# Peer routing search: picks in PSUM, 64 candidates per head, a paired first query step and key scores three pieces late

## The chip, the cores and the metric

The kernel runs on one core of one Trainium2 chip. The metric is the device time of one execution in microseconds (us). A core has TensorE (PE, matmuls, with its weight loads shown as PEld), VectorE (DVE), ScalarE (ACT), GpSimd (POOL) and SyncE (SP, which here only starts the transfers of the weight stream). Each engine works through its own instructions in the order in which the program gives them, and semaphores tie the engines together.

## The reference, cut to what matters

Two transformer blocks run one after the other over 256 tokens of width 1024. The change lies in the last part of the second block, a product-key expert layer:

```
def _peer(h, w_q, subkeys, w_down, w_up):        # h: tokens x 1024
    q = (hblk @ w_q).reshape(B, TB, 8, 2, 128)
    s = jnp.einsum('btphd,phnd->btphn', q, subkeys)      # 8 heads x 2 halves x 128 keys
    v, i = lax.top_k(s, 16)
    cand = (v[..., 0, :, None] + v[..., 1, None, :]).reshape(..., 256)
    cidx = (i[..., 0, :, None] * 128 + i[..., 1, None, :]).reshape(..., 256)
    tv, tj = lax.top_k(cand, 16)
    eidx = jnp.take_along_axis(cidx, tj, axis=-1)
    w = jax.nn.softmax(tv, axis=-1)
    a = jax.nn.gelu(jnp.einsum('btd,btpkd->btpk', hblk, w_down[eidx]))
    return jnp.einsum('btpk,btpkd->btd', w * a, w_up[eidx])
```

There are 128 x 128 experts. The kernel does not gather the chosen ones. It computes `gelu(h @ w_down.T)` for all of them in 128 tiles of 128 experts, multiplies each tile by the routing weight of every (expert, token) pair, which is zero where the expert was not chosen, and multiplies by `w_up`.

## The kernel before, in words

All weights come as one stream of 529 pieces of 128 x 1024 float32 (512 KB each), through a ring of three buffers. SP starts the transfer of piece q + 3 when the low part of piece q is done. Each piece is split into a rounded high part `wh` (ACT, L201) and a low part `wl` = piece - `wh` (L208, on DVE or, with `low=G`, on POOL). PE multiplies with three products per tile: high x high, low x high, high x low (`mm3`, L253 to L255). Three buffers of `wh` and `wl` exist (`AHEAD = 3`): ACT may write the high part of piece q + 3 only after PE has used piece q (semaphore `s_used`), and PE may start piece q only when `s_low` says that its low part is there. A piece of the query projection or of a `down` tile is 24 matmuls of 256 columns (8 slices k of the contraction x 3 products).

The part that the change touches runs in this order on PE.

1. **Operand.** `rms_operand(1, ...)` normalizes x, turns it and makes the high and low operand `xh`, `xl`, two slices k at a time (L360, L362, L366, L372). Only then, after `release()`, does POOL start the transfer of the 1 MB of sub-keys (`ld_keys`, L142).
2. **Query stage.** The loop at L1944 has 17 steps. Step st does the query piece `ph = st` (`feature_piece`, 24 matmuls into bank 0 or 1), ACT copies the result to `qp` (L1954), then PE multiplies the queries of `ph = st - 1` with their 128 sub-keys (4 instructions in the rows for the two token blocks, L1962), ACT copies the scores (L1966) and DVE searches the 16 largest of 128 for each of the two token blocks (`max`, `max_index`, `match_replace`, `max`, `max_index`: L1971 to L1978). After the loop PE waits for all score copies.
3. **Lead tiles.** 36 `down` tiles (`lead_tile`) follow, of which 0 to 5 are written out, 6 to 29 run in a loop and 30 to 35 are written out. ACT applies the gelu (L2003). The low parts of this stage and of the query stage are made by POOL. Meanwhile DVE does the routing: index conversion (L2021), sums of 16 x 16 candidates per head (L2028), top 16 of 256 for 8 heads x 2 token blocks (L2031 to L2038), softmax pieces (L2042, ACT's exp L2045), places split into row and column (L2047 to L2050), and then the picks: for row and column, and for each token block, a compare with 0..15 (L2060), a multiply by the indices (L2062) and a sum (L2064), each over 2048 elements per partition, all in SBUF. The exp stands in ACT's order behind the loop, that is behind the gelu of tile 29. Then come the sum of the weights, the reciprocal and the scaling (L2066 to L2071).
4. **Turn.** Before tile 33 PE transposes the picked indices and the weights (`turn_route`, L2078), ACT copies them out (L2081), and DVE makes the one-hot tiles (L2102, L2103).
5. **Route loop.** From the end of tile 35 on, 64 groups of four tokens are expanded by PE (L2120) beside 64 more `down` tiles, with the low parts made by DVE. Then the remaining tiles are weighed and multiplied with `w_up`.

## Time and profile before

| what | value |
|---|---|
| median of 3 runs | 1870.27 us (1869.08 to 1873.82) |
| the profiled execution, its own time | 1867.74 us |
| its span, first to last instruction | 1866.4 us |
| mean granted TensorE clock | 0.974 |
| busy: PE / DVE / ACT / POOL | 1751.0 / 1282.6 / 903.4 / 231.9 us |
| operand stage and query stage | 983.75 to 1054.5 us |
| lead tiles until the turn | 1054.5 to 1159.2 us |

Busy times are shares of a span with many stages, so they do not say which engine sets the end of one stage. That is read from stretches of the span and from the order of the instructions in the stretch. A granted clock of 1.00 is TensorE's level of 2.4 GHz, 0.50 that of 1.2 GHz.

### The profile page before, as it was taken

The page shows a single profiled execution, that of the slowest core. Times are in us where ns is not written, and L with a number is a line of the kernel's source. Part 1 is how long each engine was busy: PE and PEld are TensorE (multiplying, and loading weights), DVE is VectorE, ACT ScalarE, POOL GpSimd, SP SyncE. Part 2 cuts the span into 40 slices and gives each one's busy share as a digit, 9 for nine tenths or more (in the row PEclk, how much of TensorE's full clock was granted, in tenths as well). Part 3 has the DMA queues.
Part 4 walks back from the last instruction along what each step waited for, and adds up shares of the span by engine and source line. Part 5 has one row for each costly group of instructions (what it writes and reads, how often), then busy time and mean ns, then how long its engine had stood idle before and what let it go on. Part 6 is the DMA issues. An engine that isn't in the chain of part 4 may idle for free.

```text
span 1866.4 us, 31955 instructions
## 1 busy us (share of the span) xinstructions
PE 1751.0 (94%) x11408; PEld 1573.2 (84%) x11408; DVE 1282.6 (69%) x2300; ACT 903.4 (48%) x1584; POOL 231.9 (12%) x147
## 2 busy tenths in 40 slices
PE   7988999989989999898887998999999999999997
PEld 6757998768879987797777998999999998888885
DVE  5376866775768666767655998777786666666665
ACT  4734443455544434546444444777774443333332
POOL 1020000001110000022103799100000000000000
PEclk9989999999999999999988999999999999999999
DMA  7534756644536675444223454444445555555553
GB/s 270 199 112 138 263 180 239 237 158 145 170 119 237 216 255 194 140 147 136 80 90 114 154 173 153 146 143 137 146 138 165 184 186 185 187 186 190 191 184 120
DMA packets 85893, 317.56 MB, mean 170 GB/s; under 512 B 9568, under 2 KB 9840, under 8 KB 85024
## 3 DMA queue, kind: packets, MB, share of 16 engines
q1 hardware_dynamic: 76464, 278.43, 44.6%
q10 hardware_dynamic: 7776, 26.50, 4.0%
q0 software_dynamic: 1552, 11.25, 1.6%
q8 instruction: 67, 1.10, 0.2%
q14 instruction: 34, 0.28, 0.1%
HBM read 315.08 MB, written 1.05 MB: 169 GB/s over the span
## 4 chain that ended last, share of the span: by engine, by line
PE 77%; DVE 8%; ACT 5%; issue 4%; DMA 3%; POOL 3%; POOLq 0%; ACTq 0%; SPq 0%; DVEq 0%
PE bank L253 23%; PE bank L255 22%; PE bank L254 22%; PE bank L2120 3%; POOL wl L208 2%; DVE wl L208 2%; ACT wh L201 2%; DMA ada<-in_w_ada 1%; PE bank L493 1%; DMA ring<-in_stream 1%; PE bank L346 1%; PE bank L563 1%; PE bank L528 1%; DVE ada L334 1%; PE bank L527 0%
## 5 line engine op out<-in xcount | busy, mean ns | idle before, releaser
L201 ACT ACTIVATE wh<-ring 128x1024 fp32r<-128x1024 f32 x529 | 559.0, 1059 | 778.0 <-PE bank L255 702.8
L208 DVE TENSOR_TENSOR wl<-ring,wh 128x1024 fp32r<-128x1024 f32 x477 | 583.8, 1227 | 448.6 <-ACT wh L201 448.5
L253 PE MATMUL bank<-xh,wh 128*128 128x256 f32 x2072 | 599.1, 289 | 14.2 <-POOL wl L208 7.3
L255 PE MATMUL bank<-xh,wl 128*128 128x256 f32 x2072 | 589.3, 284 | 0.0
L254 PE MATMUL bank<-xl,wh 128*128 128x256 f32 x2072 | 589.2, 284 | 0.0
L253 PEld LDWEIGHTS bank<-xh,wh 128*128 128x128 f32 x2072 | 400.7, 193 | 20.7 <-issue 9.1
L254 PEld LDWEIGHTS bank<-xl,wh 128*128 128x128 f32 x2072 | 400.4, 193 | 1.2
L255 PEld LDWEIGHTS bank<-xh,wl 128*128 128x128 f32 x2072 | 399.9, 193 | 0.0
L253 PE MATMUL bank<-wh,wa_high 128*128 128x512 f32 x512 | 202.4, 395 | 2.1 <-DVE weighted L2139 1.4
L255 PE MATMUL bank<-wh,wa_low 128*128 128x512 f32 x512 | 201.9, 394 | 0.0
L254 PE MATMUL bank<-wl,wa_high 128*128 128x512 f32 x512 | 201.9, 394 | 0.0
L253 PE MATMUL bank<-wh,xh 128*128 128x256 f32 (+1 forms) x400 | 133.5, 334 | 25.4 <-DVE wl L208 10.7
L208 POOL TENSOR_TENSOR wl<-ring,wh 128x1024 fp32r<-128x1024 f32 x52 | 145.1, 2806 | 32.7 <-ACT wh L201 32.5
L254 PE MATMUL bank<-wl,xh 128*128 128x256 f32 (+1 forms) x400 | 129.7, 324 | 0.0
L255 PE MATMUL bank<-wh,xl 128*128 128x256 f32 (+1 forms) x400 | 129.3, 323 | 0.0
L253 PEld LDWEIGHTS bank<-wh,wa_high 128*128 128x128 f32 x512 | 96.6, 189 | 24.0 <-DVE weighted L2139 1.6
L255 PEld LDWEIGHTS bank<-wh,wa_low 128*128 128x128 f32 x512 | 96.4, 188 | 22.3
L254 PEld LDWEIGHTS bank<-wl,wa_high 128*128 128x128 f32 x512 | 96.4, 188 | 21.6 <-issue 0.2
L253 PEld LDWEIGHTS bank<-wh,xh 128*128 128x128 f32 x400 | 78.6, 197 | 36.0 <-DVE wl L208 12.6
L142 POOL DMA_DIRECT2D ring<-in_g_final x1 | 0.6, 573 | 667.8 <-DVE wl L208 667.8
L255 PEld LDWEIGHTS bank<-wh,xl 128*128 128x128 f32 x400 | 78.6, 197 | 5.4
L254 PEld LDWEIGHTS bank<-wl,xh 128*128 128x128 f32 x400 | 78.9, 197 | 5.1 <-issue 0.2
(417 smaller groups left out, 2316.0 us busy)
## 6 DMA issues: line engine op xcount, KB each, us to landing
ring<-in_stream SPq DMA_DIRECT2D x529, 512.0 KB, 3.4
ada<-in_w_ada ACTq DMA_DIRECT2D x48, 512.0 KB, 4.4
rows<-in_rows POOLq DMA_DIRECT2D x1, 2560.0 KB, 10.7
con<-in_early POOLq DMA_DIRECT2D x1, 2078.0 KB, 9.1
rows<-in_rows POOLq DMA_DIRECT2D x2, 1024.0 KB, 5.6
x_feature_major<-in_x_fm ACTq DMA_DIRECT2D x4, 256.0 KB, 8.0
x<-in_x_tm POOLq DMA_DIRECT2D x1, 1024.0 KB, 7.9
weighted<-in_subkeys POOLq DMA_DIRECT2D x1, 1024.0 KB, 8.3
```

Of the source, the lines that this page charges most:

```text
L142: engine.dma_start(dst, src).then_inc(sem, 16)
L201: C.activation(wh[q % AHEAD][:, :], ring[slot][:, :], ACT.Copy).then_inc(s_high, 1)
L208: low.tensor_tensor(wl[q % AHEAD][:, :], ring[slot][:, :], wh[q % AHEAD][:, :], ALU.subtract).then_inc(s_low, 1)
L253: T.matmul(o, left[0], right[0], start=start, stop=False, skip_group_check=True)
L254: T.matmul(o, left[0], right[1], start=False, stop=False, skip_group_check=True)
L255: return T.matmul(o, left[1], right[0], start=False, stop=stop, skip_group_check=True)
L334: ada["done"].append(dve.did(V.tensor_tensor_reduce(out=t[:, :], in0=t[:, :], in1=ada["silu_c"][:, :], scale=1.0, scalar=0.0, op0=ALU.mult ...
L346: last = T.transpose(dst_banks[k // 2][:, (k % 2) * S + t * P:(k % 2) * S + (t + 1) * P], src[:, t, k * P:(k + 1) * P], ident)
L493: T.matmul(o, v[0], w[:, 0:S], start=first, stop=False, skip_group_check=True)
L528: scored = pe.did(T.matmul(b[:, P:3 * P], q[:, P:2 * P], k, start=True, stop=True, skip_group_check=True))
L563: last = T.transpose(b[:, c * P:(c + 1) * P], pr[u % 3][:, c * P:(c + 1) * P], ident)
L2120: last = T.matmul(bank[g % 4][:, k * P:(k + 1) * P], oh_i[g % 2][:, k, :], oh_j[g % 2][:, k, :], start=True, stop=True, skip_group_check=True)
```

## The change

- **Query stage.** Query pieces 0 and 1 run as a pair: for each slice k PE does the three products of both pieces, and only then goes on to the next slice. The low parts of the two pieces that are prepared behind the pair are made by DVE, later ones by POOL as before. The queries rotate through banks 0, 1 and 7 and through four `qp` tiles. The key scores of head half ph run three pieces behind its query piece, so the loop has 19 steps, of which the last three do the lead tiles 0, 1 and 2 in place of a query piece.
- **Candidates.** With both score lists sorted, only pairs whose rank product allows it can be among the 16 largest sums. The change takes 64 of the 256 pairs: row 0 with 16 columns, rows 1 to 3 with 8, rows 4 to 7 with 4, rows 8 to 15 with 1. The row scores are read from bank 7, into which ACT copies them after tile 5 (where ACT waits for the end of the key search); ACT also converts the key indices there.
- **Places.** A place among 64 is turned into its row (`order`) and column (`place`) by 15 DVE instructions of 256 elements, in place of two shifts and masks and a conversion.
- **Picks.** The 2048-element work tile of the picks lies in PSUM banks 0 to 3, and the places that it is compared with in bank 7. The softmax subtraction comes behind the picks.

The diff, cut:

```diff
+    QB = [bank[0], bank[1], bank[7]]
+    def feature_pair(dst):
+        q = pos["q"]
+        T.wait_ge(s_low, q + 2)
+        for k in range(KD):
+            need_x(k)
+            for i in range(2):
+                h, l = wh[(q + i) % AHEAD], wl[(q + i) % AHEAD]
+                last = mm3(dst[i], (h[:, k * P:(k + 1) * P], l[:, k * P:(k + 1) * P]), (xh[:, k, :], xl[:, k, :]),
+                           k == 0, k == KD - 1)
+                if k == KD - 1:
+                    last.then_inc(s_used, 1)
+        pos["q"] = q + 2
+        split(q + AHEAD)
+        split(q + 1 + AHEAD)
+        return (s_used, q + 2)
-    for st in range(2 * PH + 1):
+    for st in range(2 * PH + 3):
         ph = st
+        if ph == 0:
+            pair_done = feature_pair([QB[0][:, 0:S], QB[1][:, 0:S]])
+        elif 2 <= ph < 2 * PH:
+            pe.wait(moved.get(ph - 3))
+            if ph == 2:
+                G.wait_ge(s_low, pos["q"] + AHEAD)
+            y = feature_piece(QB[ph % 3][:, 0:S], low=G)
+        elif ph >= 2 * PH:
+            lead_tile(ph - 2 * PH, None)
         if ph < 2 * PH:
-            act.wait(y, scored.get(ph - 2))
-            moved[ph] = act.did(C.activation(qp[ph % 2], b[:, 0:S], ACT.Copy))
-        ph = st - 1
+            act.wait(y if ph >= 2 else pair_done, scored.get(ph - 4))
+            moved[ph] = act.did(C.activation(qp[ph % 4], QB[ph % 3][:, 0:S], ACT.Copy))
+        ph = st - 3
...
-    pe.wait(*copied.values())
...
-    for u in range(BODY):
+    for u in range(3, BODY):
         lead_tile(u, None)
+    act.wait(moved[2 * PH - 1], top[2 * PH - 1])
+    rows = bank[7].rearrange("p (n w k) -> p n w k", w=2, k=TOPK)
+    turned_in = act.did(C.activation(bank[7], V16.rearrange("p t n k -> p (t n k)"), ACT.Copy))
+    ci = act.did(C.activation(I16f, I16, ACT.Copy))
...
-    ci = dve.did(V.tensor_copy(I16f, I16))
+    NC_ = 64
+    for lo, n_a, n_b in ((0, 1, 16), (1, 3, 8), (4, 4, 4), (8, 8, 1)):
+        m = dve.did(V.tensor_tensor(cand[:, :, at:at + n_a * n_b].rearrange("p n (a b) -> p n a b", b=n_b),
+                                    rows[:, :, 0, lo:lo + n_a].unsqueeze(3).broadcast_to([P, NT * PH, n_a, n_b]),
+                                    cols[:, :, 1, 0:n_b].unsqueeze(2).broadcast_to([P, NT * PH, n_a, n_b]), ALU.add))
...
+    place, order = bank[7][:, 0:S], bank[7][:, S:2 * S]
+    also = bank[0][:, 0:S]
+    m = dve.did(V.tensor_copy(place, TJ.rearrange("p n k -> p (n k)")))
+    m = dve.did(V.tensor_scalar(count, place, 16.0, None, ALU.is_ge))
+    for edge in (24.0, 32.0, 40.0, 44.0, 48.0, 52.0):
+        m = dve.did(V.scalar_tensor_tensor(count, place, edge, count, ALU.is_ge, ALU.add))
+    m = dve.did(V.scalar_tensor_tensor(order, place, -48.0, count, ALU.add, ALU.max))
...
-    c3 = cand.rearrange("p h (a b) -> p (h a) b", a=TOPK)
+    c3 = banks[:, 0:4 * HALF].rearrange("p (n k) -> p n k", k=TOPK)
+    c4 = banks[:, 0:4 * HALF].rearrange("p (h k a) -> p h k a", h=PH, a=TOPK)
-            pos_ = ABf[:, w, t, :, :].rearrange("p h k -> p (h k)").unsqueeze(2).broadcast_to([P, PH * TOPK, TOPK])
+            pos_ = places[w][:, t * P:(t + 1) * P].unsqueeze(2).broadcast_to([P, PH * TOPK, TOPK])
             m = dve.did(V.tensor_tensor(c3, pos_, io16, ALU.is_equal))
             m = dve.did(V.tensor_tensor(c4, c4, idx_, ALU.mult))
             picked = dve.did(V.tensor_reduce(IJ[:, w, t, :, :], c4, AX.X, ALU.add))
+    s1 = dve.did(V.tensor_tensor(W3, TV, TV[:, :, 0:1].broadcast_to([P, NT * PH, TOPK]), ALU.subtract))
+    act.wait(s1)
+    e_ = act.did(C.activation(Wt, Wt, ACT.Exp))
```

## Rows read from the trace of the kernel before

**Rows 1.** Windows: length, busy PE, PEld, DVE, ACT, POOL; clock, DMA share, GB/s

```profile
991.30:994.70 3.40, 3.40 (x16) 3.21 (x16) 2.71 (x4) 1.42 (x3) 0.64 (x1) 0.51 0.02 5
...
997.90:1002.46 4.56, 0.13 (x2) 0.03 (x1) 0.00 (x0) 1.33 (x2) 3.30 (x2) 0.91 0.78 291
1002.46:1008.60 6.14, 6.14 (x29) 6.14 (x30) 3.03 (x16) 0.38 (x1) 0.00 (x0) 0.51 0.28 93
1008.60:1054.50 45.90, 44.40 (x373) 44.02 (x371) 40.35 (x213) 22.82 (x43) 32.51 (x14) 1.00 0.44 146
1054.50:1107.50 53.00, 52.91 (x438) 52.68 (x439) 50.72 (x164) 24.46 (x36) 45.42 (x18) 1.00 0.52 172
1107.50:1159.10 51.60, 44.29 (x356) 42.82 (x355) 47.53 (x17) 22.61 (x33) 50.89 (x16) 1.00 0.43 144
...
1175.00:1403.00 228.00, 228.00 (x1939) 228.00 (x1938) 177.98 (x298) 170.16 (x486) 0.00 (x0) 1.00 0.42 140
```

**Rows 2.** Timeline of PE: start, length, instruction, count, idle time before

```profile
990.06 0.35 PE L253 MATMUL bank<-xh,wh 128*128 128x256 f32 x1 [1.70 <-DVE xl L372]
...
997.75 0.28 PE L255 MATMUL bank<-xh,wl 128*128 128x256 f32 x1
...
1053.32 0.71 PE L1962 MATMUL bank<-weighted 128*128 128x128 f32 x4 [1.03 <-ACT weighted L1954]
1054.55 0.35 PE L253 MATMUL bank<-xh,wh 128*128 128x256 f32 x1 [0.52 <-ACT weighted L1966]
...
1159.25 0.82 PE L2078 MATMUL bank<-keep,weighted 128*128 128x128 f32 x6
```

**Rows 3.** Waits, 985 to 1062 us: who for whom, total, times, longest

```profile
PE bank L1962 <- DMA weighted<-in_subkeys: 4.4, 1, 4.4
```

**Rows 4.** Waits, 1062 to 1175 us

```profile
ACT wh L201 <- DMA ring<-in_stream: 28.8, 11, 3.4
...
PE bank L253 <- POOL wl L208: 7.3, 7, 1.3
```

**Rows 5.** Timeline of POOL, lead tiles

```profile
1105.32 2.40 POOL L208 TENSOR_TENSOR wl<-ring,wh 128x1024 fp32r<-128x1024 f32 x1 [0.42 <-ACT wh L201]
1108.20 49.34 POOL L208 TENSOR_TENSOR wl<-ring,wh 128x1024 fp32r<-128x1024 f32 x14 [0.48 <-ACT wh L201]
```

**Rows 6.** Chain that ended last, in order of time: sub-keys, one step's scores

```profile
994.07 8.26 DMA weighted<-in_subkeys
...
1018.64 0.44 PE bank L1962 x4
```

**Rows 7.** Single lines: duration ns min/median/max, first and last start us

```profile
L2062 DVE TENSOR_TENSOR weighted<-weighted x4: 4358/4365/4385, 1110.4 to 1143.8; 128x2048 f32<-128x2048 f32 x4
```

**Rows 8.** Timeline around one POOL instruction: DVE reads a bank beside it

```profile
841.35 1.02 POOL L556 TENSOR_SCALAR ss_p<-ss_p,ss_rec 128x256 f32<-128x256 f32 x1 [9.46 <-DVE ss_rec L551]
841.48 0.68 DVE L1425 TENSOR_TENSOR rope_n<-bank,con 128x512 f32<-128x512 f32 x1
```

**Rows 9.** Timeline of DVE: searches of 128 and of 256, picks, weights

```profile
1056.73 0.28 DVE L1971 MAX8 weighted<-weighted 128x8 f32<-128x128 f32 x1
...
1058.30 0.28 DVE L1971 MAX8 weighted<-weighted 128x8 f32<-128x128 f32 x1
...
1084.32 0.43 DVE L2031 MAX8 weighted<-weighted 128x8 f32<-128x256 f32 x1
...
1086.58 0.41 DVE L2031 MAX8 weighted<-weighted 128x8 f32<-128x256 f32 x1
...
1108.04 2.29 DVE L2060 TENSOR_TENSOR weighted<-weighted,keep 128x2048 f32<-128x2048 f32 x1
...
1153.40 4.29 DVE L2071 TENSOR_TENSOR weighted<-weighted 128x128 f32<-128x128 f32 x2
```

**Rows 10.** Timeline of ACT: the exp behind tile 29

```profile
1150.91 1.28 ACT L2045 ACT_TABLE_LOAD   x1
1152.20 0.42 ACT L2045 ACTIVATE weighted<-weighted 128x256 f32<-128x256 f32 x1
```

More of the change, by code:

```diff
@@ L143, in load @@
         return (sem, 16)
-    bank = [base.enter_context(nc.psum_tensor(f"bank{i}", [P, HALF], F32))[:, :] for i in range(8)]
+    banks = base.enter_context(nc.psum_tensor("bank", [P, 8 * HALF], F32))
+    bank = [banks[:, i * HALF:(i + 1) * HALF] for i in range(8)]
     keep = sb(base, "keep", [P, KEEP["_size"]])
@@ L1935, in build @@
     ld_keys = load(G, keys, a["subkeys"], "subkeys")
-    qp = [carve(S) for i in range(2)]
+    qp = [carve(S) for i in range(4)]
     sc1 = [carve(NT, NE) for i in range(2)]
@@ L1941, in build, with down, products @@
     I16f = carve(NT, 2 * PH, TOPK)
+    s_gelu = nc.alloc_semaphore("gelu_done")
+    q0 = pos["q"] + 2 * PH
+    def down(q, s, u, n, first=False):
+        if not first:
+            T.wait_ge(s_gelu, n + (u - 2))
+        def products(h, l):
+            for k in range(KD):
+                last = mm3(bank[4 + u % 3][:, 0:S], (h[:, k * P:(k + 1) * P], l[:, k * P:(k + 1) * P]),
+                           (xh[:, k, :], xl[:, k, :]), k == 0, k == KD - 1)
+            return last
+        piece_ops(q, s, products)
@@ L1942, in build, with lead_tile @@
+    def lead_tile(u, i):
+        n = 0 if i is None else i * BODY
+        down(q0 + u, n, u, n, first=i is None and u < 3)
+        split(q0 + u + AHEAD, i, low=G)
+        C.wait_ge(s_used, n + (q0 + u + 1))
+        row = WA[:, u, :] if i is None else WA[:, bass.ds(n + u, 1), :].rearrange("p a t -> p (a t)")
+        C.activation(row, bank[4 + u % 3][:, 0:S], ACT.Gelu_apprx_tanh).then_inc(s_gelu, 1)
     top = {}
     moved, scored, copied = {}, {}, {}
-    for st in range(2 * PH + 1):
-        ph = st
-        if ph < 2 * PH:
-            b = bank[ph % 2]
-            pe.wait(moved.get(ph - 2))
-            if ph == 0:
-                G.wait_ge(s_low, pos["q"] + AHEAD)
-            y = feature_piece(b[:, 0:S], low=G)
-            act.wait(y, scored.get(ph - 2))
-            moved[ph] = act.did(C.activation(qp[ph % 2], b[:, 0:S], ACT.Copy))
-        ph = st - 1
+    QB = [bank[0], bank[1], bank[7]]
@@ new lines, in feature_pair @@
+    def feature_pair(dst):
+        q = pos["q"]
+        T.wait_ge(s_low, q + 2)
+        for k in range(KD):
+            need_x(k)
[9 more added lines that the diff above has]
+        return (s_used, q + 2)
@@ L1961, in build @@
         for t in range(NT):
-            last = T.matmul(b2[:, t * P:(t + 1) * P], qp[ph % 2][:, t * P:(t + 1) * P], keys[:, ph, :],
+            last = T.matmul(b2[:, t * P:(t + 1) * P], qp[ph % 4][:, t * P:(t + 1) * P], keys[:, ph, :],
                             start=True, stop=True, skip_group_check=True)
@@ L2039, in build @@
-    dve.wait(m)
-    for t in range(NT):
-        s1 = dve.did(V.tensor_tensor(Wt[:, t, :, :], TV[:, t, :, :], TV[:, t, :, 0:1].broadcast_to([P, PH, TOPK]),
-                                     ALU.subtract))
-    act.wait(s1)
-    e_ = act.did(C.activation(Wt, Wt, ACT.Exp))
-    V.tensor_scalar(AB[:, 0, :, :, :], TJ, 4, None, ALU.logical_shift_right)
-    m = dve.did(V.tensor_scalar(AB[:, 1, :, :, :], TJ, TOPK - 1, None, ALU.bitwise_and))
-    dve.wait(m)
-    m = dve.did(V.tensor_copy(ABf, AB))
@@ new lines, in build @@
+    dve.wait(m)
+    for n in range(NT * PH):
+        m = dve.did(V.max(TV[:, n, 0:8], cand[:, n, :]))
+        dve.wait(m)
+        V.max_index(TJ[:, n, 0:8], TV[:, n, 0:8], cand[:, n, :])
+        m = dve.did(V.match_replace(cand2, TV[:, n, 0:8], cand[:, n, :], -3.0e38))
+        dve.wait(m)
+        m = dve.did(V.max(TV[:, n, 8:16], cand2))
+        dve.wait(m)
+        m = dve.did(V.max_index(TJ[:, n, 8:16], TV[:, n, 8:16], cand2))
+    dve.wait(m)
+    place, order = bank[7][:, 0:S], bank[7][:, S:2 * S]
@@ new lines, in build @@
+    dve.wait(m)
+    V.tensor_scalar(also, order, 4.0, 24.0, ALU.mult, ALU.add)
+    m = dve.did(V.tensor_scalar(start_, order, 8.0, 8.0, ALU.mult, ALU.add))
+    dve.wait(m)
+    m = dve.did(V.scalar_tensor_tensor(start_, order, 16.0, start_, ALU.mult, ALU.min))
+    dve.wait(m)
+    m = dve.did(V.scalar_tensor_tensor(start_, order, 48.0, start_, ALU.add, ALU.min))
+    dve.wait(m)
+    m = dve.did(V.tensor_tensor(start_, also, start_, ALU.min))
+    dve.wait(m)
+    m = dve.did(V.tensor_tensor(place, place, start_, ALU.subtract))
```

56 lines of the change are left out of this document (15 added, 41 removed).

## The prediction, made blind

> **What bounds the kernel now.** I read the windows of the second block first, then PE's own timeline at their edges, then the waits, and last the instructions of DVE and POOL one by one. Times "at" are us from the start of the span of before.
>
> In the route loop and behind it PE is busy for 228.00 of 228.00 us at clock 1.00 [rows 1]. Nothing there waits, so whatever the stretch ahead of it saves should arrive at the end in full. What can be saved is where PE is idle or slow between 990 and 1160. A piece or tile of 24 matmuls takes 2.88 us at full clock: low parts that POOL makes in step with PE start at 1105.32 and 1108.20 [rows 5]. The key scores of one step take 0.44 [rows 6]. By this rule 16 query pieces and their scores need 16 x 2.88 + 16 x 0.44 = 53.1 us. They take from 990.06 to 1054.55, 64.5 us [rows 2]. The 11.4 us over are four things. The first two pieces end at 997.87 (the last matmul begins at 997.75, and matmuls follow each other by 0.12) [rows 2], 7.8 us in place of 5.8, because the operand comes two slices at a time and the clock is at 0.51 from 991.3 to 994.7 [rows 1]: 2.0 us. Then PE stands until 1002.46 for the sub-keys [rows 1, 3], whose transfer starts at 994.07 and takes 8.26 [rows 6]: 4.6 us. After this pause the clock is at 0.51, the 1.2 GHz level, for 6.14 us [rows 1], in which one score step and one piece run that need 3.32 at full clock: 2.8 us. At the end the last score step waits for ACT's copy (1.03), runs 0.71 in place of 0.44, and tile 0 waits 0.52 for the last score copy [rows 2]: 1.8 us. The rest of the stage has no gap: 44.40 busy of 45.90 us, nearly all of the rest being this end [rows 1].
>
> The 33 lead tiles up to the turn need 33 x 2.88 = 95.0 us and take from 1054.55 to 1159.25 = 104.7 [rows 2]. The 9.7 us over lie behind 1107.5, where PE is busy 44.29 of 51.60 us, against 52.91 of 53.00 ahead of it [rows 1]. There POOL is the bound: 14 low parts take 49.34 us, 3.52 each against 2.40 alone [rows 5], which is 14 x (3.52 - 2.88) = 9.0 us. PE's own waits name POOL for 7.3 us; ACT waits 28.8 us for ring transfers [rows 4], which start only when a low part is done, so they are late because POOL is. POOL is late because DVE and POOL exclude each other when a DVE instruction has two inputs in SBUF: the multiply of the picks takes 4.37 us every time [rows 7], where the first compare, which came before POOL's instruction, takes 2.29 for as many elements [rows 9].
>
> **The change, part by part.**
>
> *Pair.* PE has 12 matmuls for each two slices of the operand in place of 6, so it fills the waits. At 0.12 us up to 991.3 it does 10 of its 48, at 0.213 (16 in 3.40 us [rows 1]) up to 994.7 another 16, then 22 at 0.12: end at 997.34, 0.5 us sooner. Behind it ACT and DVE make two pieces in a row: high parts end near 998.3 and 999.3, low parts near 999.6 and 1000.8. Piece 2 is ready and runs to 1000.22, piece 3 starts there (margin 0.6 us), piece 4 at 1003.5. DVE has no search yet, so these two low parts delay nothing.
>
> *Scores three pieces late.* PE now does pieces 2 and 3, to 1003.1, before it needs the sub-keys, which were there at 1002.46. Waiting (4.6) and the slow clock behind it (2.8) are gone. The margin is only 0.6 us. From the first scores, at 1003.54 done, 15 steps of 2.88 + 0.44 follow: 12 query pieces and tiles 0, 1, 2, to 1053.3. The last score steps are covered by tiles, so the 1.8 us at the end are gone too. DVE needs 2 x 1.57 = 3.15 us for the two searches of a step [rows 9], under 3.32, so it is through at about 1057, not later than before. Sum of the stage: 0.5 + 4.6 + 2.8 + 1.8 = 9.7 us.
>
> *ACT waits for the key search behind tile 5.* Behind this wait on ACT stand two copies (some 1.2 us) and the high part and gelu of tile 6, and behind them POOL and PE. ACT comes there at 1053.3 + 3 x 2.88 + 1.4 = 1063.4, 6 us after DVE is through: no cost. The two copies fit into ACT's pause within a tile (24.46 busy of 53.00 us in the first 18 tiles [rows 1]). DVE starts its sums at 1064.0 in place of 1061.6; it has room, as follows.
>
> *Search of 64.* A search of 256 is 2.26 us, one of 128 is 1.57 [rows 9], so 64 is 1.57 - 0.345 = 1.23. Sixteen take 19.7 us, not 36.2. Sums: 1024 elements in four instructions, about 1.7. Places: 15 instructions of 256 elements at 0.41 (a `max` of 256, [rows 9]) are 6.4 us. Picks: eight compares and multiplies and four sums over 2048 elements at 2.33 start to start are 28 us. That is 1064.0 + 1.7 + 19.7 + 6.4 + 28 = 1119.8, then the subtraction, at most 2.5 with a wait for POOL. ACT reads it only behind tile 29, which PE ends at 1053.3 + 27 x 2.88 = 1131.1; high part and gelu make 1132.5, table load and exp 1.28 + 0.42 [rows 10] make 1134.2. Then sum, reciprocal and scaling take 5.1 as before (the scaling alone 4.29 [rows 9]): 1139.3. PE is at the turn at 1053.3 + 30 x 2.88 = 1139.7. So DVE's shorter work is in itself worth nothing: the exp stands behind tile 29 in ACT's order. It makes 10 us of room.
>
> *Picks in PSUM.* This is the part that gives time back to POOL. Compare and multiply then have one input in SBUF and one in a bank, and write a bank. The trace of before shows DVE reading a bank beside a busy POOL at full speed: 0.68 us for 512 elements, and POOL's instruction has its 1.02 [rows 8]. It shows no DVE instruction that writes PSUM. Bounds: it writes as fast as it writes SBUF and keeps out of POOL's way, then the 9.7 us are regained; or POOL is held up as before, then none of them is. I take the first, since the nearest row has the inputs of the new instructions, and keep 0.3 back for the scaling and for transfers that come late by chance: 9.4 us.
>
> The Trainium skill, page "SBUF — State Buffer", section "Who interferes with whom", says that a VectorE instruction with at most one SBUF input, outside the 2-port modes, does not contend with GpSimd. That agrees with the row of the bank reader; that a bank as destination is as harmless no run here shows yet. By the rule the sum is the one below; by the other bound it is 9.4 us less, which is the first rival.
>
> Behind the turn the four one-hot instructions still have two SBUF inputs and still meet POOL, so that short stretch stays as it is.
>
> **Sum.** 9.7 + 9.4 = 19.1 us. Against the profiled execution's own time: 1867.74 - 19.1 = 1848.6. That execution is 2.5 under the median of the three runs shown, so the forecast for a median is 1870.27 - 19.1 = 1851.2. A measurement of this kernel tells about 0.3%, 5.6 us, from no change.
>
> **Rivals.**
>
> *POOL stays locked out.* If the picks hold POOL up although their tile is in PSUM, the lead tiles lose their 9.4 us as before, only sooner: gain 9.7, time 1860.6. For it speaks that no row shows a bank as destination; against it the bank reader. Chance 0.08.
>
> *The front is only half regained.* The sub-keys have 0.6 us of margin and share the DMA engines with two ring transfers; low part 3 has 0.6. If the keys land 2 us later, PE pauses 1.4 and may fall to the 1.2 GHz level again for up to 2.8: gain 19.1 - 4.2 = 14.9, time 1855.4. For it: both margins are thin. Against it: the ring transfers start at nearly the same moments as before. Chance 0.09.
>
> *Writing PSUM is slow, and the kernel gets slower.* If the eight compares and multiplies take w us each, the subtraction comes 8 x (w - 2.29) later. The first 10 us are free, so it costs from w = 3.5 on; it cancels the whole gain at 8 x (w - 2.29) = 29, w = 5.9. At 8 us each it is 46 - 10 - 19 = 17 slower, 1887. ACT then sits in the wait ahead of the exp and PE runs out of high parts. Nothing in the trace speaks for it but the lack of a row. Chance 0.03.
>
> *No effect.* The gain is taken back behind the turn, say because the stream sets the pace there: 1870. The DMA share of 0.42 in the route loop with PE always busy [rows 1] speaks against it. Chance 0.03.
>
> **How the numbers follow.** The likeliest case has 0.77, with its own range of 16 to 22 us of gain, 1848 to 1854.5. Median of it: 1851. To leave out no more than 2 in 10 the range reaches over the half regained front to the locked POOL: 1847 to 1861. Faster by over 0.3%: 0.94 (all but the last two cases); within: 0.03; slower: 0.03.
>
> **What would show it.** Right: PE's first key scores follow the fourth query piece with no wait for the sub-keys; clock 1.00 from about 995 on; no gap between the last scores and a tile; every low part of POOL about 2.4 us while the picks run, compares and multiplies 2.3 us, tiles 2.88 apart; DVE idle for about 10 us before the weights' sum, released by ACT's exp; the turn at 1140 in place of 1159; the stretch behind it as long as before. Wrong: low parts of 4.4 us beside the picks; compares over 3.5 us; a wait for the sub-keys with a slow clock behind; PE waiting for ACT's high parts around the exp.

## The result, and the profile after

Over six runs each the changed kernel has a median of 1852.44 us (1842.48 to 1858.05), the kernel before 1869.67 (1864.19 to 1876.42). The ratio is 0.9903 with a 95% interval of 0.9882 to 0.9924, so the gain is 18.1 us, and between 14.2 and 22.1. The forecast was a gain of 19.1 and a time of 1851 in 1847 to 1861.

The profiled execution of the changed kernel is the slowest of its six, 1858.05 us, with a span of 1856.8. It reaches the stage of the change later than the profiled execution of before did: the transfer of the sub-keys starts at 1005.88 in place of 994.07 [rows 6], 11.81 us later, and in both kernels the first query product comes 4.0 us ahead of it. Nothing that was changed runs before that. The second profile of this very kernel, below, has the transfer at 996.68. So places are compared after 11.81 is taken off.

Windows of the changed kernel: stretch, its length, busy time of PE, PEld, DVE, ACT and POOL with the number of instructions, granted clock, DMA share, GB/s.

```profile
1003.10:1006.50 3.40, 3.40 (x20) 3.40 (x20) 2.73 (x4) 1.43 (x3) 0.62 (x1) 0.61 0.00 0
1006.50:1009.70 3.20, 3.20 (x29) 3.20 (x28) 0.00 (x0) 0.38 (x1) 0.02 (x1) 1.00 0.74 248
...
1015.20:1065.10 49.90, 49.90 (x423) 49.90 (x423) 42.58 (x225) 25.48 (x46) 36.55 (x16) 1.00 0.50 167
1065.10:1151.75 86.65, 86.65 (x725) 86.65 (x724) 60.87 (x195) 44.22 (x66) 71.60 (x31) 1.00 0.54 178
...
1166.00:1393.00 227.00, 227.00 (x1931) 227.00 (x1930) 177.87 (x299) 169.92 (x484) 0.00 (x0) 1.00 0.43 142
```

PE's own timeline: the third piece, the first key scores, the turn, the first two route products.

```profile
1009.40 0.28 PE L254 MATMUL bank<-xh,wh 128*128 128x256 f32 x1
...
1015.16 0.61 PE L2009 MATMUL bank<-weighted 128*128 128x128 f32 x4
...
1151.80 0.82 PE L2123 MATMUL bank<-keep,weighted 128*128 128x128 f32 x6
1161.08 1.09 PE L2165 MATMUL bank<-onehot_j,onehot_i 128*128 128x128 f32 x8
1164.88 1.05 PE L2165 MATMUL bank<-onehot_j,onehot_i 128*128 128x128 f32 x8
```

The third piece follows the pair and the key scores follow the fourth piece with no bracket of idle time. The pause for the sub-keys and the 1.2 GHz stretch behind it [rows 1, 3] are gone. From there to the turn PE is busy in every microsecond, where in the last 51.60 us ahead of the turn it was busy 44.29 before [rows 1]. The first scores come at 1015.16, which is 1003.35 on the clock of before (forecast 1003.1), the turn at 1139.99 (forecast 1139.7, before 1159.25 [rows 2]).

DVE's compare and multiply of the picks, and beside them POOL's low parts, from the two timelines:

```profile
1104.31 2.30 DVE L2101 TENSOR_TENSOR bank<-bank,keep 128x2048 f32<-128x2048 f32 x1
1106.64 2.30 DVE L2103 TENSOR_TENSOR bank<-bank,weighted 128x2048 f32<-128x2048 f32 x1
```

```profile
1104.17 2.41 POOL L209 TENSOR_TENSOR wl<-ring,wh 128x1024 fp32r<-128x1024 f32 x1 [0.47 <-ACT wh L202]
1107.05 2.42 POOL L209 TENSOR_TENSOR wl<-ring,wh 128x1024 fp32r<-128x1024 f32 x1 [0.47 <-ACT wh L202]
```

The rows that were missing from the trace of before are now there: an instruction of DVE that writes a bank takes 2.30 us for 2048 elements, as much as the undisturbed one in SBUF [rows 9], and POOL's low part beside it takes 2.41 and comes every 2.88 us, where before 14 took 49.34 [rows 5]. The waits from 1065 to 1166 us (who for whom, total, times, longest) have no line in which PE waits:

```profile
ACT wh L202 <- PE bank L256: 48.8, 33, 1.7
POOL wl L209 <- ACT wh L202: 17.6, 33, 1.1
DVE weighted L2111 <- ACT weighted L2109: 13.7, 1, 13.7
```

ACT now waits for PE, and its 28.8 us of waiting for the ring [rows 4] are gone. DVE idles 13.7 us ahead of the weights' sum. Two things were not forecast. The sub-keys' transfer was quicker than in before, 5.6 us in place of 8.3. And the stretch behind the turn became shorter: turn to second product is 13.1 us, before 15.2. The one-hot instructions there show why:

```profile
1154.04 2.11 DVE L2147 TENSOR_TENSOR onehot_i<-keep,route_i 128x512 f32<-128x512 f32 x1 [6.35 <-ACT route_j L2126]
1156.07 0.68 DVE L2148 TENSOR_TENSOR onehot_j<-keep,route_j 128x512 f32<-128x512 f32 x1
1156.67 0.68 DVE L2147 TENSOR_TENSOR onehot_i<-keep,route_i 128x512 f32<-128x512 f32 x1
1157.27 2.89 DVE L2148 TENSOR_TENSOR onehot_j<-keep,route_j 128x512 f32<-128x512 f32 x1
```

Two of the four take 0.68. In before they took 2.11, 2.89, 2.87 and 2.89. POOL's low parts and ACT's first high part behind the turn, in the changed kernel and then in before:

```profile
1156.74 8.13 POOL L209 TENSOR_TENSOR wl<-ring,wh 128x1024 fp32r<-128x1024 f32 x3 [1.14 <-ACT wh L202]
...
1152.06 1.06 ACT L202 ACTIVATE wh<-ring 128x1024 fp32r<-128x1024 f32 x1 [1.55 <-PE bank L256]
```

```profile
1161.74 8.00 POOL L208 TENSOR_TENSOR wl<-ring,wh 128x1024 fp32r<-128x1024 f32 x3 [1.58 <-ACT wh L201]
...
1160.61 1.06 ACT L201 ACTIVATE wh<-ring 128x1024 fp32r<-128x1024 f32 x1 [2.65 <-DMA ring<-in_stream]
```

POOL pauses once in both, and now the pause (1155.60 to 1156.74) lies where the second and third one-hot start, while in before it was over at 1161.74, ahead of the first one at 1162.59. The place of the pause comes from ACT. In before ACT's high part starts 1.36 us behind the turn, because a ring transfer, late through POOL, ends its wait. Now it starts 0.26 us behind the turn, and the copies and the one-hots behind it are 1.1 us sooner too.

**A measure for the stage.** The place of the stage moves by up to 12 us between executions, while what follows the second route product took 691.84 to 691.97 us in every profile taken. So T below is the time from the start of the issue of the sub-keys' transfer to the start of the second route product. Before has 180.40, the changed kernel 159.00 and, profiled again, 159.01. The stage became 21.4 us shorter: 19.3 up to the turn, 2.1 behind it. One thing moves T without any edit: the clock in the first two query pieces, which lie around its start. The pair took 7.52 us here, with the clock at 0.61 in the window above, and 5.82 in the two profiles below in which it ran at 1.00 throughout. That is 1.7 us of T. The time from the first scores to the turn is free of it.

### The profile page after: what moved, and what is told of

Its sections match the earlier page's. It is cut to its first block, busy times and chain, and to the rows that moved or that the text cites. A ratio compares the mean times of both kernels' runs of the same rounds, so it can differ in the third digit from the quotient of the medians.

```text
span 1856.8 us, 31972 instructions
## 1 busy us (share of the span) xinstructions
PE 1757.8 (95%) x11408; PEld 1581.0 (85%) x11408; DVE 1242.8 (67%) x2314; ACT 904.7 (49%) x1586; POOL 207.9 (11%) x145
## 4 chain that ended last, share of the span: by engine, by line
PE 84%; DVE 7%; ACT 4%; DMA 2%; issue 2%; POOL 0%; ACTq 0%; DVEq 0%; SPq 0%; POOLq 0%
PE bank L254 25%; PE bank L255 25%; PE bank L256 25%; PE bank L2165 3%; DVE wl L209 2%; ACT wh L202 1%; DMA ada<-in_w_ada 1%; PE bank L494 1%; PE bank L347 1%; PE bank L529 1%; PE bank L564 1%; DVE ada L335 1%; PE bank L528 0%; PE bank L495 0%; PE bank L692 0%
## 5 line engine op out<-in xcount | busy, mean ns | idle before, releaser
L209 POOL TENSOR_TENSOR wl<-ring,wh 128x1024 fp32r<-128x1024 f32 x50 | 121.0, 2420 | 37.4 <-ACT wh L202 37.3
L2156 ACT ACTIVATE onehot_j<-onehot_j,route_w 128x128 f32<-128x128 f32 x256 | 81.4, 397 | 0.0
```

The source lines that it names most:

```text
L209: low.tensor_tensor(wl[q % AHEAD][:, :], ring[slot][:, :], wh[q % AHEAD][:, :], ALU.subtract).then_inc(s_low, 1)
L2156: last = C.activation(row, row, ACT.Copy, scale=wT[:, TB * g + k:TB * g + k + 1])
```

## The experiments

Diffs are against the changed kernel and cut to their main lines. "Ratio" is to the kernel before, timed on the same chip.

**One half alone: the front.** The pair and the late scores, with the search of 256 and the picks in SBUF as in before; the index conversion and the softmax subtraction stand where they stood.

```diff
-    NC_ = 64
-    cand = carve(NT * PH, NC_)
+    cand = carve(PH, TOPK * TOPK)
...
+    ABf = carve(2, NT, PH, TOPK)
...
-    c3 = banks[:, 0:4 * HALF].rearrange("p (n k) -> p n k", k=TOPK)
+    c3 = cand.rearrange("p h (a b) -> p (h a) b", a=TOPK)
```

> The query stage of the change (pair, scores three behind, tiles 0 to 2 in the loop) with the whole routing search of before (256 candidates, all in SBUF). Measure T, from the start of the sub-keys' transfer on POOL to the start of the second route product on PE: 180.4 us before (994.07 to 1174.47), 159.0 after (1005.88 to 1164.88). Theory A (the parts lean on each other: DVE's chain of before takes 97.7 us from the end of the key search to the scaled weights, and the key search ends only 2.9 us sooner, so DVE now sets the turn): PE waits for DVE's weights ahead of the turn, gain 4 to 5 us, T about 176, whole time 1864 to 1866 against before 1870. Theory B (the parts add, as my sum had it): 9.7 us less, T about 170.7, time 1860.

Measured: 1866.58 us over ten runs, ratio 0.998 (0.9957 to 1.0002), T 173.8. The interval includes 1, so the time by itself shows no gain. T is 6.6 us less than before, but this is one of the two profiles with the pair at full clock:

```profile
994.80:997.00 2.20, 2.20 (x18) 2.20 (x19) 2.02 (x4) 2.04 (x5) 0.00 (x0) 1.00 0.00 0
```

With the pair at 7.5 us as in the changed kernel T would be 175.5 and the gain 4.9 (an estimate from the two durations), where the front by itself was sized at 9.7. This is theory A. DVE's, POOL's and PE's timelines at the turn:

```profile
1150.17 2.29 DVE L2087 TENSOR_REDUCE weighted<-weighted 128x128 f32<-128x2048 f32 x1
...
1153.10 4.07 DVE L2094 TENSOR_TENSOR weighted<-weighted 128x128 f32<-128x128 f32 x2
...
1132.41 24.62 POOL L209 TENSOR_TENSOR wl<-ring,wh 128x1024 fp32r<-128x1024 f32 x7
```

```profile
1152.51 0.66 PE L2101 MATMUL bank<-keep,weighted 128*128 128x128 f32 x4 [1.28 <-DVE weighted L2087]
1157.23 0.69 PE L2101 MATMUL bank<-keep,weighted 128*128 128x128 f32 x2 [4.06 <-DVE weighted L2094]
```

PE comes to the turn sooner and then waits 1.28 us for the last pick and 4.06 for the scaled weights. Up to the turn the front does bring what it was sized at: 165.2 us from the transfer's start before, 153.7 here, and 1.7 of the difference is the clock of the pair. Behind the turn 4.9 us are lost again. DVE, with the long search and picks of 4.4 us, is now last, and its two scaling instructions take 4.07 us beside a POOL that works without a pause. The same two take 0.49 in the changed kernel, where they begin in a pause of POOL (1146.89 to 1147.44):

```profile
1147.19 0.49 DVE L2116 TENSOR_TENSOR weighted<-weighted 128x128 f32<-128x128 f32 x2
```

So the two halves of the change need each other: the front alone runs into DVE, and DVE into POOL.

**The other half alone: search and picks.** The query stage of before (one piece at a time, scores one behind) with the new search.

```diff
-    for st in range(2 * PH + 3):
+    for st in range(2 * PH + 1):
...
-        if ph == 0:
-            pair_done = feature_pair([QB[0][:, 0:S], QB[1][:, 0:S]])
-        elif 2 <= ph < 2 * PH:
+        if ph < 2 * PH:
...
-        ph = st - 3
+        ph = st - 1
```

> The query stage of before with the routing search of the change (64 candidates, places and picks in PSUM). Theory A: the wait for the sub-keys (4.6 us), the slow clock behind it and the wait at the end of the stage come back, POOL is free in the lead tiles: T (sub-keys' transfer to second route product) about 159.0 + 9.7 - 0.5 = 168 to 169 us, every low part of POOL 2.4 us, time 1860. Theory B (what POOL regained is lost again because the stage in front sets the end): T over 174.

Measured: 1861.77 us over ten runs, ratio 0.9943 (0.9919 to 0.9966), T 170.3. POOL's low parts are all at 2.4. PE's timeline at the first and the last key scores and at tile 0:

```profile
1013.59 1.20 PE L1963 MATMUL bank<-weighted 128*128 128x128 f32 x4 [5.63 <-DMA weighted<-in_subkeys]
...
1063.67 0.71 PE L1963 MATMUL bank<-weighted 128*128 128x128 f32 x4 [1.03 <-ACT weighted L1955]
1064.90 0.36 PE L254 MATMUL bank<-xh,wh 128*128 128x256 f32 x1 [0.52 <-ACT weighted L1967]
```

and the windows behind each of these two places:

```profile
1013.59:1019.70 6.11, 6.11 (x36) 6.11 (x37) 3.04 (x16) 0.96 (x2) 0.00 (x0) 0.66 0.13 54
...
1064.90:1069.00 4.10, 4.10 (x22) 4.10 (x23) 3.82 (x21) 0.00 (x0) 0.88 (x1) 0.58 0.51 180
```

T is 11.3 over that of the whole change and 10.1 under that of before. It is the four losses of the old query stage again, with other sizes. From the first scores to the turn PE took 147.9 us for work that at full clock needs 14 x 2.88 + 16 x 0.44 + 33 x 2.88 = 142.4: 2.0 for the clock behind the pause (its first two scores are 5.28 us apart where a step takes 3.32), the 1.8 at the end, and a loss that before did not have, the clock at 0.58 over the 4.10 us behind the two small waits, in which 16 products follow each other by 0.213 in place of 0.12: 1.5. The transfer of the sub-keys took 9.2 us here, so the pause was 5.6 in place of 4.4 [rows 3]. Theory A named the losses rightly, 168 to 169 was a little low.

**Everything of the change but PSUM.** The work tile and the two lists of places in SBUF.

```diff
-    places = (order, place)
+    at_sb = carve(2, S)
+    V.tensor_copy(at_sb[:, 0, :], order)
+    m = dve.did(V.tensor_copy(at_sb[:, 1, :], place))
...
+    places = (at_sb[:, 0, :], at_sb[:, 1, :])
-    c3 = banks[:, 0:4 * HALF].rearrange("p (n k) -> p n k", k=TOPK)
+    c3 = carve(4 * HALF).rearrange("p (n k) -> p n k", k=TOPK)
```

> The changed kernel with the 2048-element work tile and the places of the picks back in SBUF, 64 candidates kept. Theory A (POOL is locked out by DVE instructions with two SBUF inputs, and that is what the lead tiles lose): compares and multiplies 4.4 us, POOL's low parts beside them 3.5 us in the mean, lead tiles lose 8 to 9 us: T about 167 to 168, time 1861. Theory B (what counts is that DVE has less to do, through 64 candidates): T stays at 159 to 160, because DVE has over 10 us of room.

Measured: 1860.52 us over ten runs, ratio 0.994 (0.9918 to 0.9962), T 169.5. Single lines (shortest, median, longest in ns), then the waits from 1060 to 1172 us:

```profile
L2106 DVE TENSOR_TENSOR weighted<-weighted,keep x4: 3670/4394/4395, 1101.5 to 1134.3; 128x2048 f32<-128x2048 f32 x4
...
L2108 DVE TENSOR_TENSOR weighted<-weighted x4: 4357/4368/4383, 1105.2 to 1138.7; 128x2048 f32<-128x2048 f32 x4
```

```profile
ACT wh L202 <- DMA ring<-in_stream: 25.0, 9, 3.2
...
PE bank L254 <- POOL wl L209: 6.9, 7, 1.3
```

The pattern of before is back [rows 4, 7], although the search is short: 8.7 us between the first scores and the turn, and 1.9 behind the turn, where the one-hots again take 2.11, 2.89, 2.88 and 2.88 and ACT's high part again waits for the ring. Theory A came true.

**Everything of the change but the 64 candidates.** The picks in PSUM, the search of 256, with the places, the index conversion and the softmax subtraction of before.

```diff
-    NC_ = 64
-    cand = carve(NT * PH, NC_)
-    cand2 = carve(NC_)
+    cand = carve(PH, TOPK * TOPK)
+    cand2 = carve(PH, TOPK * TOPK)
...
+    ABf = bank[7].rearrange("p (w t h k) -> p w t h k", w=2, t=NT, h=PH)
```

> The query stage of the change with the search of before over 256 candidates in SBUF, and only the places and the work tile of the picks in PSUM. Theory A (fewer candidates are worth nothing by themselves, since the exp stands behind tile 29 in ACT's order and DVE's picks end at about the same moment, 1133 against 1134 us in the time of before): T 159 to 161, time as the changed kernel. Theory B (the 64 candidates are needed, DVE comes too late without them): each us by which DVE is late shows as a wait of PE ahead of the turn, T 163 or more.

Measured: 1852.71 us over six runs, ratio 0.9919 (0.9887 to 0.9951), T 159.3 against 159.0. The wait of 13.7 us that DVE had ahead of the weights' sum is nearly used up, and still comes last on ACT's exp:

```profile
1138.48 0.42 DVE L2090 TENSOR_REDUCE weighted<-weighted 128x16 f32<-128x256 f32 x1 [1.94 <-ACT weighted L2068]
```

The fourfold smaller search is worth 0.3 us in T, and nothing that the whole time can tell, once the picks are in PSUM. With the picks in SBUF it is worth more: 175.5 (the front alone, with the pair's clock taken out) against the 169.5 of the run above.

**Which of the two operands counts.** First the work tile alone in SBUF, the places in their bank; then the places alone in SBUF, the work tile in PSUM.

```diff
-    c3 = banks[:, 0:4 * HALF].rearrange("p (n k) -> p n k", k=TOPK)
+    c3 = carve(4 * HALF).rearrange("p (n k) -> p n k", k=TOPK)
```

> The changed kernel with only the work tile of the picks in SBUF; the places stay in PSUM. So the compare has one SBUF input and writes SBUF, the multiply has two SBUF inputs. Theory A (the inputs decide): compares 2.3 us, multiplies 4.4 us, POOL loses half of what it lost, nearly all of it inside its own slack: T 159 to 162. Theory B (the place of the work tile decides, output included): compares 4.4 us too, T about 167.

```diff
-    places = (order, place)
+    places = (at_sb[:, 0, :], at_sb[:, 1, :])
```

> The changed kernel with the places copied to SBUF ahead of the picks; the work tile stays in PSUM. So the compare has two SBUF inputs and writes PSUM, the multiply has one. Theory A (the inputs decide): compares 4.4 us where they meet POOL, multiplies 2.3 us, T 159 to 162. Theory B (a bank as destination keeps DVE out of POOL's way): both 2.3 us, T 159.

Each was run once: 1854.69 us with T 160.4, and 1854.15 with T 162.1. Compare and multiply of the first kernel, then of the second:

```profile
L2102 DVE TENSOR_TENSOR weighted<-bank,keep x4: 2291/2291/2291, 1099.5 to 1124.8; 128x2048 f32<-128x2048 f32 x4
...
L2104 DVE TENSOR_TENSOR weighted<-weighted x4: 2291/4480/4492, 1101.8 to 1127.1; 128x2048 f32<-128x2048 f32 x4
```

```profile
L2105 DVE TENSOR_TENSOR bank<-weighted,keep x4: 3673/4440/4449, 1097.9 to 1124.6; 128x2048 f32<-128x2048 f32 x4
...
L2107 DVE TENSOR_TENSOR bank<-bank,weighted x4: 2299/2299/2299, 1101.6 to 1129.1; 128x2048 f32<-128x2048 f32 x4
```

Of the four kinds of instruction, the two with both inputs in SBUF take 4.4 us and the two with one input in a bank 2.3, whether they write a bank or SBUF. The inputs decide, the destination doesn't. The loss up to the turn is small, 1.4 and 1.2 us, because only four instructions are long, in place of eight. The second kernel loses another 1.9 behind the turn: there ACT's high part waits 2.11 us for the ring, and all four one-hots are long.

**The distance of the scores.** Two pieces behind in place of three; then one piece behind, with the pair kept.

```diff
-    for st in range(2 * PH + 3):
+    for st in range(2 * PH + 2):
...
-        ph = st - 3
+        ph = st - 2
```

> The changed kernel with key scores two pieces behind the queries. PE then comes to the sub-keys 2.9 us sooner, about 2.2 us ahead of their landing. Theory A (the third piece is what covers the transfer): PE waits about 2.2 us for the sub-keys and the clock stays at 1.00: T about 161. Theory B: after the pause the clock falls to 0.5 as in the kernel before, up to 2.8 us more: T about 164.

Measured: 1850.62 us in one run, T 158.9. The sub-keys had landed in 5.2 us, before PE came to the scores, so the run shows no pause, and neither theory is tested. What it does show is that one step less of distance costs nothing when the transfer is quick.

```diff
-    for st in range(2 * PH + 3):
+    for st in range(2 * PH + 1):
...
-        ph = st - 3
+        ph = st - 1
```

> The changed kernel with key scores one piece behind the queries, as before, and the pair kept. PE comes to its first scores about 3.7 us behind the start of the sub-keys' transfer, which took 5.2 to 9.2 us in the runs so far, so it waits 1.5 to 5.5 us. Theory A (the pause costs its own length only): T is 159.0 plus the wait, plus some 1.8 us for the end of the stage. Theory B (the clock falls behind the pause): up to 2.8 us on top, with the granted clock at 0.5 for about 6 us behind the wait.

Measured: 1862.15 us in one run, T 166.1. PE's timeline at the first scores, and the windows behind it:

```profile
1011.06 1.19 PE L2009 MATMUL bank<-weighted 128*128 128x128 f32 x4 [4.53 <-DMA weighted<-in_subkeys]
```

```profile
1011.06:1014.50 3.44, 3.44 (x16) 3.44 (x17) 1.70 (x9) 0.38 (x1) 0.00 (x0) 0.50 0.58 220
1014.50:1017.50 3.00, 3.00 (x20) 3.00 (x20) 1.34 (x8) 0.42 (x1) 0.00 (x0) 0.69 0.00 0
```

T grew by 7.1, and only 4.5 of it is the pause. From the first scores to the turn there are 144.8 us for 142.4 of work, 2.4 more, and the clock row shows where: 1.2 GHz for 3.44 us and part of the next 3.00, while PE was never idle. Here the pause costs its own length and then half as much again (theory B). The 1.8 us for the end of the stage, which both theories counted in, did not come: tile 0 now runs ahead of the last scores.

**Without the pair.** Pieces 0 and 1 one after the other, all else as in the change.

```diff
-        if ph == 0:
-            pair_done = feature_pair([QB[0][:, 0:S], QB[1][:, 0:S]])
-        elif 2 <= ph < 2 * PH:
+        if ph < 2 * PH:
```

> The changed kernel without the pair: query pieces 0 and 1 one after the other, scores three behind. Theory A (the pair fills the waits for the operand, worth 0.5 us): T 159.5. Theory B (the pair costs, since both high parts can be remade only at its end): T under 159.0.

Measured: 1850.14 us in one run, T 158.9 against 159.0. The first two pieces took 7.44 us one after the other and 7.52 as a pair. In both profiles they began at 1.2 GHz, and PE had no wait between two products that a second piece could have filled. So the pair is worth nothing at that clock. What it is worth at 2.4 GHz no two runs compare.

**Warm-up products.** What is left is the stretch at 1.2 GHz around the first pieces. Extra products of old operands into an unused bank, ahead of the transposes of the normed input, keep PE busy there. The first kernel has them at one place, the second at four.

```diff
+WARM = 40
...
+        if which:
+            for _ in range(WARM):
+                T.matmul(bank[3][:, 0:S], xh[:, 0, 0:P], xh[:, 0, :], start=True, stop=True, skip_group_check=True)
```

> The changed kernel with 40 extra matmuls of 256 columns into a bank that nobody reads, put on PE ahead of the transposes of the operand stage, where PE idles 4.7 us for the normalized x. The output is the same. Theory A (the low clock of the operand stage comes from this idle time): the clock is 1.00 for the transposes and the pair, transposes 1.9 us in place of 3.7, the pair 5.8 to 6.2 in place of 7.5, some 3 us less from the end of the last output piece to the end of the pair. Theory B (the operand's arrival sets the pace, not the clock): under 1 us. A third way: the extra matmuls outlast the idle time and push the transposes back.

Measured: 1849.7 us in one run, T 157.3. PE's timeline of it, then the row of the changed kernel that answers to its second row:

```profile
986.36 4.96 PE L1316 MATMUL bank<-xh 128*128 128x256 f32 x40
991.21 1.97 PE L348 MATMUL bank<-keep,x_normed 128*128 128x128 f32 x16
```

```profile
996.77 3.67 PE L347 MATMUL bank<-keep,x_normed 128*128 128x128 f32 x16 [4.68 <-ACT x_normed L1307]
```

The transposes are nearly twice as fast. T is not the measure here, since it starts behind them. From the end of the last output piece to the end of the pair it is 14.5 us in place of 17.3, so theory A's 3 us came (the next expectation has 12.9 for it, which the profile does not bear out). Of these 2.8 the transposes bring 1.1, because PE waits 2.06 us for the first operand behind them in place of 1.44. The other 1.7 are the pair at full clock, and that the warm-up did not earn for certain: the front alone has it with no warm-up, and the four-place kernel, with one, does not. Windows of the first pieces, one place and then four:

```profile
995.20:999.00 3.80, 3.77 (x31) 3.80 (x32) 3.20 (x6) 2.56 (x5) 0.00 (x0) 1.00 0.02 4
```

```profile
989.68:993.00 3.32, 3.32 (x20) 3.32 (x21) 2.72 (x5) 2.53 (x5) 0.00 (x0) 0.69 0.00 0
```

The four-place kernel was timed beside an unchanged copy of the changed kernel, both over six runs:

```diff
+        n_, b_ = {"ln1_g0": (34, 7), "ln1_g1": (34, 5)}.get(g, (0, 0))
+        turned = turn_halves(z, turn_banks, (n0, n0), n1, n_, b_)
...
+        turned = turn_halves(dst, banks, (n0, n0), n1, *((38, 3) if which else (28, 5)))
```

> The changed kernel with extra matmuls (34, 34, 28 and 38 of 256 columns into a bank that nobody reads) on PE ahead of the transposes at four places where PE idles 3.6 to 4.7 us for a normalized x and then runs at the low clock: the first layer norm of both layers of the first block, and both rms norms of the second block. The output is the same. With only the last of the four, the stretch from the last output piece to the end of the pair was 12.9 us in place of 17.3. Theory A (the low clock behind each pause is what costs): 3 to 4.5 us less at each of the four places, in all 12 to 16 us under the changed kernel, time about 1838, mean clock near 0.98, ratio to the changed kernel 0.992 to 0.994. Theory B (elsewhere the operand's arrival sets the pace): only the last place gains, time about 1848.

> The changed kernel once more, as the measure for the kernel with the extra matmuls. Median 1850 to 1854, ratio to before 0.990; T 158.9 to 159.1 if the stage is as steady as its single profiles have it.

Measured: 1845.31 us with the four warm-ups, ratio 0.9869 (0.9847 to 0.9891), and 1848.89 for the copy, ratio 0.9887 (0.9863 to 0.9912). The intervals overlap; the medians are 3.6 us apart, where the theory that the clock is what counts there said 12 to 16. The two profiles tell where it went. From the last product ahead of each of the four places to the 49th behind its transposes the warm-ups save 2.6, 0.0, 0.9 and 1.2 us. The transposes run at full clock at all four. But then PE idles a second time, 2.06 to 4.25 us, until the first operand is made, and in or behind that idle time the clock fell at three of the four places; only the first, which saves most, stayed at 1.00. So warm-ups ahead of the transposes do not cover the second idle time. The four-place kernel has the lowest median of all, but the lead over the changed kernel isn't established.

The copy shows how thin the distance of three pieces is: its sub-keys took 9.0 us and landed at 1005.71, and PE came to the scores at 1005.82. Its T is 159.01.

T of all profiles. "Low parts" is the mean of POOL's low parts over the whole span in ns; "keys" the time in us in which the sub-keys landed. In the two kernels that have the query stage of before, and where the scores are closer, pieces of 2.88 us that the others do ahead of the first scores lie behind them: two of them in before, in "search and picks alone" and in "one behind", one in "two behind".

| kernel | T | first scores to turn | turn to second product | low parts | keys |
|---|---|---|---|---|---|
| before | 180.4 | 156.8 | 15.2 | 2806 | 8.3 |
| changed | 159.0 | 136.6 | 13.1 | 2420 | 5.6 |
| front alone | 173.8 | 146.1 | 20.1 | 2804 | 5.4 |
| search and picks alone | 170.3 | 147.9 | 13.1 | 2417 | 9.2 |
| no PSUM | 169.5 | 145.4 | 15.0 | 2727 | 8.5 |
| 256 candidates | 159.3 | 137.0 | 13.1 | 2502 | 5.4 |
| work tile in SBUF | 160.4 | 138.1 | 13.1 | 2578 | 7.6 |
| places in SBUF | 162.1 | 137.8 | 15.0 | 2549 | 8.4 |
| scores two behind | 158.9 | 139.5 | 13.1 | 2420 | 5.2 |
| scores one behind | 166.1 | 144.8 | 13.1 | 2418 | 8.1 |
| no pair | 158.9 | 136.6 | 13.1 | 2420 | 5.3 |
| one warm-up | 157.3 | 136.6 | 13.1 | 2419 | 5.3 |
| four warm-ups | 158.8 | 136.6 | 13.1 | 2420 | 5.1 |
| changed, again | 159.0 | 136.8 | 13.1 | 2420 | 9.0 |

## Why the prediction held, step by step

**The whole.** The forecast of 19.1 us for the way to the turn met 19.3 in the profiles, and the mechanisms are those that it named. The stage as a whole gained 21.4, 2.1 of them behind the turn, where none were forecast. Over the runs the gain is 18.1 (14.2 to 22.1), and 20.2 for the copy against before beside it. That 18.1 lies so near 19.1 is therefore partly luck: the sum left out 2.1, and medians over six runs are no finer than these intervals.

**Late scores.** Right. The pause and the slow clock behind it are gone (no bracket at 1015.16), and the run with one piece of distance brings both back, 4.5 and 2.4 us. The margin of 0.6 us was rightly called thin. Landing times spread from 5.1 to 9.2 over the profiles, so 8.3, from which it was worked out, is near their upper end, and PE came to the scores 9.1 to 9.3 us behind the transfer's start. With the sub-keys 9.0 us on the way 0.1 was left. With the pair at full clock PE comes after 7.6, and a slow landing would then meet it too early by 1.6 (an estimate from 9.2 and 7.6). The rival "the front is only half regained" did not come up in any profile, but no run excludes it.

**The front's size.** The front was sized at 9.7 us. The run without it is 11.3 longer in T. Brought to the conditions of before this is 11.3 - 0.9 (its first scores came 9.33 us behind the start of the transfer, those of before 8.40) - 1.5 (the slow stretch at the end, which before did not have) + 0.8 (2.8 lost behind the pause in before, 2.0 here) = 9.7. That agrees, though it is the same account read backwards and no second test. The direct one is the front alone up to the turn: 165.2 - 153.7 - 1.7 = 9.8. The 11.3 shows how loose the term is: with a later transfer and a clock that also falls behind the end's small waits, the old stage is 1.6 slower. The forecast counted on the one execution it had.

**The pair.** Sized at 0.5 us, measured 0.1 against the run without it, which is nothing. The step that failed is "so it fills the waits". The forecast took the clock of before's execution, 1.00 for the first products and 0.51 behind them. In the profiles with and without the pair the clock was at its lower level from the first product on, and PE so slow that there were no waits to fill.

**The search of 64.** Right: it was called worth nothing in itself, and 159.3 against 159.0 shows it. But the reason given holds only as far as PSUM does the rest. In the front-alone run the long search stands with the long picks, and PE waits 1.28 + 4.06 us for DVE at the turn. Had the picks been held up, the short search would have paid, 6.0 us by 175.5 against 169.5. DVE's idle time ahead of the sum was forecast at about 10 us and is 13.67, of which the short search and the new places make 13.67 - 1.94 = 11.7. Two terms of DVE's sum were off without effect: 15 instructions at 0.41 are 6.2 and not 6.4, and the sum, reciprocal and scaling "as before", 5.1 us, took 1.2, because the scaling, 4.29 in before beside a busy POOL, takes 0.49 where it meets a pause. The parts were added in the forecast as if independent; alone they bring 4.9 (with the pair's clock taken out) and 10.1, together 21.4. Of the 6.4 us between, 4.9 are lost behind the turn when the front is changed alone, and 1.6 are what the old query stage lost more in the other run than in before.

**Picks in PSUM.** Right, the one step for which no row existed. The upper bound was the true one: 9.4 us were forecast, and the run with all in SBUF loses 8.7 up to the turn. Compare and multiply take 2.30 us, low parts 2.41, and the two mixed kernels show that what counts is the number of inputs in SBUF. By the rule cited from the Trainium skill, page "SBUF — State Buffer", section "Who interferes with whom", at most one SBUF input leaves GpSimd alone; the trace agrees, and these runs add that it holds for a bank as destination, and that two SBUF inputs contend even when a bank is written (4440 ns at L2105).

**Behind the turn.** The step that was sized wrongly: "that short stretch stays as it is". It became 2.1 us shorter. The one-hots do still have two inputs in SBUF, and two of them still meet POOL. But POOL's earlier lateness reached behind the turn through the ring: ACT's high part waited for a late transfer, and with it the route copies, the one-hots and the place of POOL's pause. Both kernels in which the places are compared from SBUF have ACT waiting for the ring there and give 1.9 us back, with no edit behind the turn; the one with only the work tile in SBUF does not. The forecast counted the freed POOL only up to the turn.

**Median and profile.** The forecast set the profiled execution of before beside its median and moved both by the same sum. That is what the median did, 1869.67 to 1852.44. The profiled pair alone would have shown 1867.74 - 1858.05 = 9.7 us, half of it, since the changed kernel's execution came to the stage 11.8 us later through work that is the same in both. Only T and the six runs tell that these 11.8 belong to the execution and not to the change.

## What to carry to other kernels

When DVE and POOL share a stage, count for each DVE instruction the inputs that lie in SBUF: moving one of two into a free bank halved it and gave POOL its time back, which was worth more than cutting the number of candidates to a quarter. A pause of PE costs more than its length, so put independent products ahead of an operand that comes by a transfer, enough of them for its slowest landing and the fastest clock. Do not add up the gains of parts that free different engines: find who is next at the joint place, and time a stage from a mark ahead of it to a mark behind it, when the work before the stage moves it by more than the change is worth, and look at the granted clock at the mark before a small difference is believed.

## What the runs showed that was not expected

- Writing a bank costs DVE nothing over SBUF: 2299 ns against 2291 for 128x2048 f32 with one input in a bank.
- The same transfer of 1024 KB on POOL's queue landed in 5.1 to 9.2 us. The changed kernel itself had 5.6 and 9.0. What makes the difference stays open.
- Two short waits of 1.03 and 0.52 us, with 0.71 us of work between, were followed by a clock of 0.58 over 4.10 us in one kernel, and by no slow stretch in the kernel before, which had the same two waits [rows 1, 2]. What tips it stays open.
- The execution-to-execution spread of this kernel comes from ahead of the stage: the start of the sub-keys' transfer lay between 993.7 and 1005.9 us in 14 profiles, and in the two of the changed kernel 9.2 us apart, the stretch behind the second route product between 691.84 and 691.97.
- Forty warm-up products brought the transposes behind them from 3.67 to 1.97 us. The last of them began 1.6 us sooner, of which 0.6 went into a longer wait for the first operand.
- Behind the same program text up to there, the pair took 5.82 us in the front alone, at clock 1.00, and 7.4 to 7.5 in the other kernels without warm-up, in part at the lower level. What decides it stays open.
